# Cached keys and rotary rows of a paged attention: transfers of two steps and of half a layer in place of one and two steps

## The reference

```python
past_ckv = cache_ckv[l, page_table].reshape(bs, past_len, KV_LORA)   # 8 x 4096 x 128
past_kr = cache_krope[l, page_table].reshape(bs, past_len, QK_ROPE)  # 8 x 4096 x 32
...
s = jnp.einsum('bthc,blc->bhtl', ql, ckv) + jnp.einsum('bthr,blr->bhtl', qr, krope)
s = s.astype(jnp.float32) * scale
s = jnp.where(qp[:, None] >= k_pos[None, :], s, -1e30)
p = jax.nn.softmax(s, axis=-1).astype(ckv.dtype)
return jnp.einsum('bhtl,blc->bthc', p, ckv)
```

## Time and profile before

| | us |
|---|---|
| median of 3 runs (1906.38 to 1908.42) | 1907.14 |
| the profiled execution, its own time | 1897.7 |
| its span | 1895.9 |
| PE busy | 1754.3 (93%) |
| DVE busy | 831.4 (44%) |
| POOL busy | 320.1 (17%) |
| `cache_scores` matmuls (line 1121, 2560), busy | 121.3 |
| key loads on POOL (line 581, 64), busy | 60.2 |

### The profile page before, as it was taken

The page is one execution under the profiler, slowest core; times in us unless marked ns, Lnnn a source line. Parts: engine busy times, 40 slices in busy tenths (PEclk is TensorE's granted clock), DMA queues, the critical chain, the costliest instruction groups (busy, mean ns, idle before and its releaser), DMA issues. The chain is left out here.

```text
span 1895.9 us, 26903 instructions
## 1 busy us (share of the span) xinstructions
PE 1754.3 (93%) x11012; PEld 1155.0 (61%) x11012; DVE 831.4 (44%) x1646; ACT 402.3 (21%) x839; POOL 320.1 (17%) x327
## 2 busy tenths in 40 slices
PE   8999989999999999999899898989999999899990
PEld 6876546788888454333378764468888874533330
DVE  4677756433332361111529576563343334511116
ACT  0126512111111121111410363121111111211111
POOL 0012221000000002364000121300000005123635
PEclk8998968999999989999999988789999999899995
DMA  9103333422222657995650222442221336699974
GB/s 278 60 25 98 121 115 115 138 62 88 84 81 92 269 231 288 416 412 218 241 155 1 70 86 90 136 143 87 89 89 56 105 117 252 264 365 413 416 276 165
DMA packets 140957, 322.57 MB, mean 170 GB/s; under 512 B 34350, under 2 KB 96548, under 8 KB 122340
## 3 DMA queue, kind: packets, MB, share of 16 engines
q1 hardware_dynamic: 103270, 204.45, 30.1%
q0 software_dynamic: 36064, 114.61, 16.7%
q10 hardware_dynamic: 1502, 1.80, 0.3%
HBM read 360.20 MB, written 29.48 MB: 206 GB/s over the span
## 5 line engine op out<-in xcount | busy, mean ns | idle before, releaser
L1234 PE MATMUL ps<-space 128*128 128x272 f32 x1024 | 250.3, 392 | 0.0
L1719 PE MATMUL ps<-space,xT 128*64 128x512 f32 x864 | 226.7, 595 | 0.0
L459 PE MATMUL ps<-xT,space 128*128 128x272 f32 (+1 forms) x960 | 224.4, 397 | 1.5 <-DMA space<-in_w_in 1.5
L1234 PEld LDWEIGHTS ps<-space 128*128 128x128 f32 x1024 | 194.6, 190 | 40.1
L459 PEld LDWEIGHTS ps<-xT,space 128*128 128x128 f32 (+1 forms) x960 | 183.3, 191 | 42.4 <-DMA space<-in_w_in 1.9
L1242 PE MATMUL ps<-space 128*128 128x272 f32 x640 | 157.1, 392 | 0.0
L1121 PE MATMUL ps<-space,fifth 32*32 32x256 f32 x2560 | 121.3, 508 | 25.2 <-DVE space L878 11.9
L1980 DVE SCALAR_TENSOR_TENSOR space<-space,ps 128x256 f32<-128x256 f32 x32 | 21.5, 672 | 269.6 <-ACT space L1821 269.6
L1242 PEld LDWEIGHTS ps<-space 128*128 128x128 f32 x640 | 121.6, 190 | 25.1
L1234 PE MATMUL ps<-xT,space 128*128 128x272 f32 x512 | 128.8, 395 | 0.0
L1719 PEld LDWEIGHTS ps<-space,xT 128*64 128x64 f32 x864 | 69.7, 137 | 90.7 <-issue 88.3
(11 more groups left out here) (385 smaller groups left out, 2234.2 us busy)
## 6 DMA issues: line engine op xcount, KB each, us to landing
space<-in_w_in SPq DMA_DIRECT2D x44, 1024.0 KB, 5.5
space<-in_exp_w_down SPq DMA_DIRECT2D x32, 1024.0 KB, 12.5
space<-in_exp_w_gate SPq DMA_DIRECT2D x30, 1024.0 KB, 10.2
space<-in_exp_w_up SPq DMA_DIRECT2D x30, 1024.0 KB, 12.2
space<-in_w_o SPq DMA_DIRECT2D x8, 1024.0 KB, 6.0
space<-x_rows SPq DMA_DIRECT2D x16, 512.0 KB, 5.9
space<-y_rows SPq DMA_DIRECT2D x16, 512.0 KB, 7.2
space<-in_p_attn SPq DMA_DIRECT2D x8, 512.0 KB, 6.4
```

What stands on the lines that cost most here:

```text
L459: t = nc.tensor.matmul(ps[0:m, 2 * (n % 4) + h, 0:HN], w[:, f, c * P:c * P + m], k.xT[:, f, h, :], start=(f == 0), stop=(f == KD - 1))
L1234: t = m.matmul(out, w[:, f, :], x[:, f, :], start=(first and f == 0), stop=(f == H - 1), skip_group_check=True)
L1719: i = m.matmul(ps[r, 6 + t % 2, :], k.xgT[:, t % 2, f, r], gate_up_of(g)[:, f], start=(f == 0), stop=(f == KD - 1), skip_group_check=True)
```

## The change

Keys are fetched sixteen a partition (8 KB, 1 MB a transfer), so that one transfer serves two steps: 16 transfers a layer in place of 32, called wide here. Rotary rows are fetched 32 keys a partition (4 KB, 512 KB a transfer), which serves the four steps of a half: 8 transfers in place of 16. There are 8 places (`KEEP`) of 1 MB: six in `stream`, one in `fifth`, one in the arena. Rotary rows have 4 places, three in `stream` and one in `fifth`.

Which keys form a step changes with it: partition r now holds keys 16 r to 16 r + 15 of a run of 2048, and a step takes the first or the second 8 of each. `first_index` finds the page among four instead of two, with more steps on DVE. `fifth` also holds state rows that SP writes out at the start of `attend`, so the loads into it wait for `s_out`, all output transfers. SP's first fill of `merge` waits for `d_pv` 12 in place of 14. The rotary transposes of step 0 move from turns 4 to 7 of the prompt's attention to turns 8 to 11. Five semaphores are added to keep their numbers in order; they do nothing else.

```diff
@@ first_index: the page among four, the row within it (ends of the new code)
+    quads = k.idxf.rearrange("p (n e) -> p n e", e=4)
...
+    for e in range(3):
+        ch.step(v.scalar_tensor_tensor(page, diff[:, :, e], late[:, e:e + 1], page, ALU.mult, ALU.add))
+        ch.settle()
...
+    ch.step(v.tensor_scalar(k.idxr[:], page, 4.0, at[:, 2:3], ALU.mult, ALU.add))
@@ sizes and loads
-UNITS = 4 * STEPS
-KEEP = 15
-AHEAD = 12
+WIDE = 2 * STEPS
+KEEP = 8
+AHEAD = 6
...
 def load_keys(k, pool, u):
-    s, b = u // 4, u % 4
-    row = (4 * (s // LOADS) + b) * LOADS + s % LOADS
+    p, b = u // 4, u % 4
+    row = (4 * (p // PAIRS) + b) * PAIRS + p % PAIRS
...
-def load_rotary(k, pool, p, b):
-    c = (p % 2) * 4 + b
-    row = (4 * (p // PAIRS) + b) * PAIRS + p % PAIRS
-    at = bass.IndirectOffsetOnAxis(ap=k.idxr[:, row:row + 1], axis=0)
-    pool.indirect_dma_start(k.ckr[c], None, k.kr_table, at).then_inc(k.c_inr[c], 16)
+def load_rotary(k, pool, h, b):
+    at = bass.IndirectOffsetOnAxis(ap=k.idxr[:, 4 * h + b:4 * h + b + 1], axis=0)
+    pool.indirect_dma_start(k.ckr[b], None, k.kr_table, at).then_inc(k.c_inr[b], 16)
@@ SP in attend
-            sp.wait_ge(*due(k, k.d_pv, 2 * (STEPS - 2) + 2))
+            sp.wait_ge(*due(k, k.d_pv, 2 * (STEPS - 3) + 2))
@@ POOL in attend
             for b in range(4):
-                load_rotary(k, pool, 0, b)
+                if b < 3:
+                    load_rotary(k, pool, 0, b)
                 load_keys(k, pool, b)
...
             for u in range(4, AHEAD):
-                if u >= 8:
-                    load_rotary(k, pool, 1, u - 8)
                 load_keys(k, pool, u)
                 pool.wait_ge(*due(k, k.c_in[u], 16))
-            pool.wait_ge(*due(k, k.c_t, 2 * TURNS))
+            pool.wait_ge(*due(k, k.s_out, 16 * (3 + 3 * DB + 8 + 4)))
+            load_rotary(k, pool, 0, 3)
+            load_keys(k, pool, KEEP - 2)
+            pool.wait_ge(*due(k, k.c_v, TURNS))
             load_keys(k, pool, KEEP - 1)
-            pool.wait_ge(*due(k, k.c_v, TURNS))
-            for u in range(AHEAD, KEEP - 1):
-                load_keys(k, pool, u)
-            for u in range(KEEP, UNITS):
-                if u in (KEEP, KEEP + 8):
-                    pair = 2 + (u - KEEP) // 8
-                    pool.wait_ge(*due(k, k.d_kr, 8 * (pair - 1)))
-                    for b in range(4):
-                        load_rotary(k, pool, pair, b)
-                pool.wait_ge(*due(k, k.d_pv, 2 * ((u - KEEP) // 4) + 2))
+            pool.wait_ge(*due(k, k.d_kr, 4 * LOADS))
+            for b in range(4):
+                load_rotary(k, pool, 1, b)
+            for u in range(KEEP, WIDE):
+                pool.wait_ge(*due(k, k.d_pv, 4 * (u // 4 - 1)))
                 load_keys(k, pool, u)
@@ DVE: a unit's keys are half of a place
-                dve.wait_ge(*due(k, k.c_in[u % KEEP], 16 * (u // KEEP + 1)))
-                v.transpose(k.kT[:, u % TURNED, :], k.ckv[u % KEEP]).then_inc(k.d_kc, 1)
+                s, b = u // 4, u % 4
+                wide = 4 * (s // 2) + b
+                dve.wait_ge(*due(k, k.c_in[wide % KEEP], 16 * (wide // KEEP + 1)))
+                v.transpose(k.kT[:, u % TURNED, :], k.ckv[wide % KEEP][:, 1024 * (s % 2):1024 * (s % 2) + 1024]).then_inc(k.d_kc, 1)
...
-                if 4 <= i < 8:
-                    turn_rotary(0, i - 4)
+                if 8 <= i < 12:
+                    turn_rotary(0, i - 8)
```

More of the change, by code:

```diff
@@ L268, in first_index @@
         if q == 0:
-            v.tensor_tensor(both, pages, mine, ALU.mult).then_inc(k.s_idx, 1)
+            ch.step(v.tensor_tensor(quads, pages, mine, ALU.mult))
         else:
[L271 to L282, removed]
@@ L283, in first_index @@
-    v.tensor_scalar(at[:, 2:3], at[:, 0:1], 2.0, 1.0, ALU.mult, ALU.add).then_inc(k.s_idx, 1)
-    dve.wait_ge(*due(k, k.s_idx, 21))
-    v.tensor_scalar(k.idxr[:], page, 8.0, at[:, 0:1], ALU.mult, ALU.add).then_inc(k.s_idx, 1)
+            ch.step(v.tensor_tensor(k.idxt.rearrange("p (n e) -> p n e", e=4), pages, mine, ALU.mult))
+            ch.settle()
+            ch.step(v.tensor_tensor(k.idxf[:], k.idxf[:], k.idxt[:], ALU.add))
+            ch.settle()
+    diff, late, at = k.idxt[:, 0:24].rearrange("p (n e) -> p n e", e=3), k.idxt[:, 24:27], k.idxt[:, 27:32]
@@ new lines, in first_index @@
+    page = quads[:, :, 0]
+    for e in range(3):
+        ch.step(v.tensor_scalar(late[:, e:e + 1], k.row[:, 0:1], 4.0 * (e + 1), None, ALU.is_ge))
+    ch.step(v.tensor_tensor(diff, quads[:, :, 1:4], quads[:, :, 0:3], ALU.subtract))
+    ch.settle()
+    for e in range(3):
+        ch.step(v.scalar_tensor_tensor(page, diff[:, :, e], late[:, e:e + 1], page, ALU.mult, ALU.add))
+        ch.settle()
+    ch.step(v.tensor_tensor(at[:, 0:1], late[:, 0:1], late[:, 1:2], ALU.add))
+    ch.settle()
+    ch.step(v.tensor_tensor(at[:, 1:2], at[:, 0:1], late[:, 2:3], ALU.add))
@@ L286, in first_index @@
+    ch.settle()
+    ch.step(v.scalar_tensor_tensor(at[:, 2:3], at[:, 1:2], -4.0, k.row[:, 0:1], ALU.mult, ALU.add))
+    ch.settle()
+    ch.step(v.tensor_scalar(at[:, 3:4], at[:, 2:3], 2.0, None, ALU.mult))
+    ch.step(v.tensor_scalar(at[:, 4:5], at[:, 2:3], 2.0, 1.0, ALU.mult, ALU.add))
+    ch.settle()
+    ch.step(v.tensor_scalar(k.idxr[:], page, 4.0, at[:, 2:3], ALU.mult, ALU.add))
     for e in range(2):
-        v.tensor_scalar(k.idx.rearrange("p (n e) -> p n e", e=2)[:, :, e], page, 16.0, at[:, 1 + e:2 + e], ALU.mult, ALU.add).then_inc(k.s_idx, 1)
@@ L288, in first_index @@
-    v.tensor_scalar(k.before[:], k.cmask[:], 0.5 * NEG, None, ALU.is_lt).then_inc(k.s_idx, 1)
+        ch.step(v.tensor_scalar(k.idx.rearrange("p (n e) -> p n e", e=2)[:, :, e], page, 8.0, at[:, 3 + e:4 + e], ALU.mult, ALU.add))
+    ch.step(v.tensor_scalar(k.before[:], k.cmask[:], 0.5 * NEG, None, ALU.is_lt))
 def projection(k, sp, l, pos):
@@ L2033, in forget_caches @@
     for i in range(KEEP):
-        pool.wait_ge(*due(k, k.c_in[i], 16 * len(range(i, UNITS, KEEP))))
-    for i in range(2 * 4):
+        pool.wait_ge(*due(k, k.c_in[i], 32))
+    for i in range(4):
         pool.wait_ge(*due(k, k.c_inr[i], 32))
@@ L2074, in build @@
         k.cmask, k.nmask = sb("cmask", [P, P]), sb("nmask", [HS, DB, 32])
-        k.row, k.pages, k.idx = sb("row", [P, 1 + 4 + 8]), sb("pages", [P, DB * NPAGE], I32), sb("idx", [P, DB * LOADS], I32)
-        k.idxr = sb("idxr", [P, DB * PAIRS], I32)
+        k.row, k.pages, k.idx = sb("row", [P, 1 + 4 + 8]), sb("pages", [P, DB * NPAGE], I32), sb("idx", [P, DB * PAIRS], I32)
+        k.idxr = sb("idxr", [P, DB], I32)
         k.idxf, k.idxt, k.pick = sb("idxf", [P, DB * LOADS]), sb("idxt", [P, DB * LOADS]), k.row[:, 5:13]
@@ L2164, in build @@
         k.krT = [kr0, kr1]
-        k.ckv = [stream[:, i * 8 * P:(i + 1) * 8 * P] for i in range(AHEAD)] + [more[:, 0], more[:, 1], last]
-        rotary = stream[:, AHEAD * 8 * P:AHEAD * 10 * P].rearrange("p (c n) -> p c n", c=6)
-        k.ckr = [rotary[:, i, :] for i in range(6)] + [sb("ckr6", [P, 512])[:], k.fifth[:, 1280:1792]]
+        places = [stream[:, i * 16 * P:(i + 1) * 16 * P] for i in (4, 5, 0, 1, 2, 3)]
+        k.ckv = places + [k.fifth[:, 2304:4352], more.rearrange("p c n -> p (c n)")]
+        k.ckr = [stream[:, (12 + i) * 8 * P:(13 + i) * 8 * P] for i in range(3)] + [k.fifth[:, 1280:2304]]
         at = queries + 4 * 2 * HN
@@ L2269, in build @@
         k.c_in = [sem(f"c_in{i}") for i in range(KEEP)]
-        k.c_inr = [sem(f"c_inr{i}") for i in range(2 * 4)]
-        k.pool_sems = k.c_in + k.c_inr
+        k.c_inr = [sem(f"c_inr{i}") for i in range(4)]
+        k.pool_sems = k.c_in + k.c_inr + [sem(f"more{i}") for i in range(5)]
         assert [s.num for s in k.pool_sems] == list(range(k.c_in[0].num, k.c_in[0].num + len(k.pool_sems)))
```

25 lines of the change are left out of this document (12 added, 13 removed).

## The result

The changed kernel takes **1874.8 us** (median of 4 runs, 1872.8 to 1876.5) against 1907.8 (4 runs, 1906.4 to 1909.0): ratio 0.983, 95% interval 0.981 to 0.984, 33 us less. The forecast was 1889.4, 18 us less. The profiled execution took 1874.9 us; its span is 22.8 us shorter than that of the earlier trace rows.

A forecast was written before the change was run, and what follows sets the result against it. PE was taken to starve in the cached steps while POOL issues runs of transfers. Steps -8.1 a layer, -16.2, and the first fill -1.5 take 1897.7 to 1880.0 us profiled, 1889.4 as median; range 1877 to 1902.

The forecast's parts named there:

- rival 2: Large key rows move faster in the cached steps: fourth load lands after 13.1 us, 1872 us in all; chance 0.18.
- S0: Cached step 0, from its start of `cache_scores` to the next: seven POOL transfers become one, 18.7 us before, -8.2.
- S3: Cached step 3: four issues instead of eight, but a new wait for keys; 19.0 us becomes 17.2, -1.8.
- S5: Cached step 5: second run of four key loads and the same landing; 12.3 us becomes 17.2, +4.9.
- S4: Cached step 4: no issues left in it; 13.5 us becomes 9.6, -3.9.
- S2: Cached step 2: four key loads become four rotary loads, as many issues; 12.9 us, change 0.
- S6: Cached step 6: PE may stand at half clock after a wait; 7.9 us before, +0.9 (between 0 and 1.7).
- S7: Last cached step and the end: change 0, at most +1 us for PE at half clock.
- Issues, not bytes: Cached steps: PE starves while POOL issues a run of transfers, about 1.2 us each; a single one costs nothing.
- Late keys: Key loads issued only when wanted: fourth 1 MB load lands 16.1 us after the first issue, at 320 GB/s.
- The first fill: First fill of `merge` starts some 8 us earlier, ending PE's 1.49 us wait: -1.5 in layer 0, 0 in layer 1.
- The same change gives 1889.4 there: Median of runs: 9.4 us above the profiled execution, so the forecast 1880.0 us becomes 1889.4.

The follow-up runs named there:

- more_issues: Changed kernel plus six further small indirect POOL transfers (128 rows of 128 bytes) behind the lone one in S0; 1898.0 us, ratio 0.996.
- half_bytes: Changed kernel with key loads for steps 4 to 7 bringing 4 KB rows instead of 8, as many issues; 1860.9 us, ratio 0.976.
- more_plain: Changed kernel plus six plain POOL transfers without an index (128 rows of 128 bytes) in S0; 1875.7 us.
- late_fill: Changed kernel with the first fill of merge waiting again for the values of step 6, not step 5; 1874.3 us.
- values_first: Changed kernel with the values of step 3 run before the scores of step 4; 1872.6 us, ratio 0.983.

## Why the prediction was right, and where not

- **The time: nearer to a rival than to the forecast.** Forecast 18 us less, measured 33. 1874.8 lies below the forecast's own range (1877 to 1902) and inside only the one widened to 1873 for rival 2, whose 1872 is the nearest number. But rival 2 had it from the steps, at -16.9 a layer, and they gave about half of that. The gain in the steps was foreseen with its cause; that the time came out where rival 2 had it is luck.
- **Steps: right.** Forecast -8.1 a layer, -16.2; measured -9.0 and -6.7, -15.7. S0 10.4 (10.5), S3 16.6 and 17.3 (17.2), S5 15.5 and 15.3 (17.2), S4 8.7 and 10.0 (9.6), S2 13.3 (12.9), S6 9.6 and 8.9 (8.8). S5 was rated 1.8 too dear, S7 1.4 and 3.0 too cheap, and the sum is as close as it is because these two cancel in part.
- **Issues, not bytes: right**, shown by more_issues and half_bytes from both sides. "A single one costs nothing" was a little too strong: around the lone issue of S0 the 160 matmuls take 4.28 us, where the forecast had 3.7, against 3.38 in S7 without one, all at a granted clock of 1.00.
- **Late keys.** The fourth landing was put at 16.1 us from 3.0 fixed and 3.3 a MB, and is 14.8. Rival 2's 13.1 was nearly as close in this term, but of its S4 and S6 at full clock only S4 of layer 0 came near (8.7); S6 did in neither layer. The Trainium skill, "DMA: Bandwidth & Descriptors", section "Anatomy of one DMA — SWDGE (gpsimd) path", has about 2.0 us plus the bytes at 436 GB/s for a transfer; the estimate from it was 11.6, and the trace, with 14.8, does not agree.
- **The first fill: wrong, -1.5 forecast, about 0 measured.** The wait goes, but S7, beside which the transfers now run, gets longer by what they save. I gave S7 "at most +1" for the clock and did not ask what the moved fill would collide with.
- **"The same change gives 1889.4 there": wrong, and the largest error.** I carried the 9.4 us between the profiled execution and the median of the kernel before over to the changed kernel. Its profiled execution is within 0.1 us of its median. On the chip where the median of before is 1898.5, more_plain, whose steps are the changed kernel's, is 22.8 us faster, just the difference of the first two spans; on the other chip, with before at 1904.8, late_fill is 30.5 us faster. The two stand at 1875.7 and 1874.3, so it is the kernel before that differs between the chips, by 6 us. On which chip its first profiled execution ran the record does not say. Runs of before spread from 1894 to 1910, with their mean granted clock between 0.937 and 0.927; those of the changed kernel and of more_plain and late_fill, whose steps are all but the same, lie between 1871 and 1879 at 0.940 and more. The slower runs have the lower clocks. Starving alone does not explain it: more_issues has longer steps than before, and yet its runs lie between 1893 and 1902 at 0.936 to 0.940, beside runs of before between 1898 and 1910 at 0.927 to 0.936. Which stage of before runs at the lower clock no trace shows, since all three are of runs at 0.933. The cause stays open.
- **The rest, 22.8 - 15.7 = 7 us of the spans**, is mostly chance of single executions: `merge` and the experts of layer 0 (from the last values of S7 to PE's first matmul of layer 1) take 618.6 us in the first trace of before, but 615.6 and 615.0 in the other two and 614.9 after. The prompt's attention of layer 1 (from its first scores to S0) takes 52.3 us after and 54.3 to 55.0 in the three of before. Fewer issues stand there, but they are not the cause: before has 52.5 in layer 0 with more of them, and values_first and half_bytes, whose loads there are the changed kernel's, have 54.9 and 54.7 in layer 1. The term stays at 0, as forecast.

## What to carry to other kernels

Count the indirect transfers that POOL issues while PE works through many tiny matmuls, and how close they follow each other; merge them, or put other work between them, so that fewer fall beside the tiny matmuls (one memset of 0.5 us took them to every 1.8 us here). Larger transfers that replace small ones land later and in step with their bytes, so ask at the same time how early their places come free. When a transfer is moved earlier to end a wait, look at what PE does in the time it now falls into. And do not add the offset between one kernel's profiled execution and its median to another kernel.
